# A hybrid decoder block on one core: the last expert chunk written out behind the loop, with the final norm beside it

## The chip, the cores and the metric

The kernel runs on one core of a Trainium2 chip. A core has TensorE (PE, matrix products), VectorE (DVE), ScalarE (ACT), GpSimd (POOL, which also issues gathers and scatters by index) and SyncE (SP, which here only issues DMAs); 16 DMA engines move the data. The engines run side by side, each works its own queue in order, and they wait for each other on semaphores. The metric is the device time of one execution in microseconds, the median of several runs.

## The reference

One decoder layer over 2048 tokens of width 1024, then a final norm:

```python
h = rmsnorm(x, norm_mix_w)
proj = h @ w_in                      # split into the inputs of two mixers
mixed = concat(gla(...), ssd(...))   # gated linear attention, state space scan
x = x + mixed @ w_out
h2 = rmsnorm(x, norm_ffn_w)
# 32 experts, each token goes to its top 4:
#   y = (clip(up) + 1) * (min(gate) * sigmoid(1.702 * gate)) @ w_down + b_down
x = x + moe_ffn(h2, ...)             # sum over the token's experts, weighted
return rmsnorm(x, final_norm_w)      # x * rsqrt(mean(x*x) + 1e-6) * w
```

All inputs and the output are float32.

## The kernel before

A first phase (mixers and router, about a third of the time) leaves two arrays in device memory: `xacc_d`, the residual stream, and `h2_d`, its normed rows. For each expert it also leaves a table of token numbers and gate weights.

The second phase is a loop over chunks. A chunk is one expert with up to 320 of its tokens; the chunks are sorted by size, and there is one loop for each of eight sizes (320, 304, ..., 208 tokens), all of them made by `chunk_loops`. In this run there are 32 chunks, and the last is of the smallest size, 208. A chunk `i` has 12 units of work, `q` = 0 to 11: units 0 to 7 are the gate and up products (128x416 and 128x208 products on `xhl`), units 8 to 11 the down products (on `ahl`). Each unit uses a 1 MB piece of weights. The precision of float32 is kept by splitting each operand in a high and a low part, and this takes three engines for each piece:

- SP: `load(e, q)` brings the piece into `raw`, a ring of four slots, once DVE has freed the slot (`v_lo`).
- ACT: `hi(i, q)` writes the high part `whi` from `raw`; DVE: `lo(i, q)` writes the low part `wlo`. Both run four units ahead of PE.
- PE: `products`; then ACT and DVE (`evict`) add the bias and the two halves. After each odd unit below 8, DVE computes the activation (`activated`), ACT its high part (`act_hi`) and DVE its low part (`act_lo`, `ahl`). The last quarter of unit 8 on PE waits for the last of these (`v_al`).

Between the units lie the token rows. `x_rows` on PE turns the gathered tokens of the NEXT chunk (in unit 8, and behind it); `x_evict`, `x_hi`, `x_lo` split them. `y_rows` turns the results `yT` of the PREVIOUS chunk back (behind units 1 and 2, in PSUM tile `tpm`), ACT scales them by the gate weights into `ybuf`, and POOL adds them to `xacc_d` by an indirect DMA (`scatter`, an accumulating write). There are two row blocks (128 and 80 rows for the smallest size), and POOL waits for the first scatter before it issues the second.

Behind the loop stands the tail: the results of the last chunk are turned (PE), scaled (ACT), scattered (POOL, two scatters one behind the other), and then SP loads all of `xacc_d` in four pieces of 2 MB into `fin` (line 590). For each of 16 tiles of 128 rows ACT squares and sums (`squares`, line 1243), POOL makes the root for four tiles at a time (lines 821 and 823: an add and a power), DVE scales (line 1827) and SP stores (line 594). `fin` takes 64 KB of each partition, which is free only when the expert buffers are.

`own_wait` (line 628) is a tiny POOL instruction in front of which POOL's waits stand.

## Time and profile before

| | us |
|---|---|
| median of 3 runs (3551.17 to 3553.92) | 3552.98 |
| the profiled execution | 3550.52 |
| its span in the trace | 3548.9 |
| PE busy (share of the span) | 3408.6 (96%) |
| DVE busy | 2147.0 (60%) |
| ACT busy | 1660.9 (47%) |
| POOL busy | 614.0 (17%) |

All times of rows are in microseconds from the start of the span. The times of the runs contain a little more than the span: 1.6 us around it in the profiled execution. In a timeline row the first number is the start, the second the duration, and a bracket says how long the engine was idle ahead of it and what ended that. "PEclk" is the TensorE clock that was granted, 1.00 being 2.4 GHz and 0.50 being 1.2 GHz; "DMA share" is the busy share of the 16 DMA engines.

### The profile page before, as it was taken

Reading aid. Unit: us, or ns where it says so; the run is one execution under the profiler, and the core shown is the slowest. Engines: PE = TensorE matmul, PEld = TensorE weight load, DVE = VectorE, ACT = ScalarE, POOL = GpSimd, SP = SyncE. Lnnn points to the kernel's source line nnn. Section 1 sums busy time; section 2 is a strip of 40 time slices with the busy share of each in tenths; the row PEclk is TensorE's granted clock in tenths of the full one; section 3 lists DMA queues with packets and bytes.
Section 4 is the critical chain, followed back from the end, with each engine's and each line's share of the span. In section 5 each row is a group of like instructions: output and inputs, shape, how many; then the busy total and the mean of one; then the engine's idle time right before and its main releaser. Section 6 shows DMA issues by size and latency. Waiting matters only on the chain.

```text
span 3548.9 us, 58966 instructions
## 1 busy us (share of the span) xinstructions
PE 3408.6 (96%) x22297; PEld 3153.4 (89%) x22297; DVE 2147.0 (60%) x2762; ACT 1660.9 (47%) x2161; POOL 614.0 (17%) x834
## 2 busy tenths in 40 slices
PE   5999999999996999999999999999999999999993
PEld 5888888888886999999999999988888999999992
DVE  3565355445455555555666666667667777777774
ACT  3443333333233444444444445455555556566664
POOL 1011111111113111111111211222112112112121
PEclk8999999999997999999999999999999999999996
DMA  9888888887865555665566666676666767768776
GB/s 340 332 306 333 299 292 286 298 306 269 300 253 187 170 169 172 180 182 178 180 191 183 205 191 188 185 218 211 203 199 214 215 204 235 223 205 242 237 235 244
DMA packets 474717, 821.53 MB, mean 231 GB/s; under 512 B 19408, under 2 KB 420960, under 8 KB 458224
## 3 DMA queue, kind: packets, MB, share of 16 engines
q1 hardware_dynamic: 442720, 716.52, 59.1%
q0 software_dynamic: 24400, 76.27, 9.3%
q10 hardware_dynamic: 7488, 27.27, 2.1%
q8 instruction: 70, 1.15, 0.1%
q14 instruction: 39, 0.32, 0.0%
HBM read 720.85 MB, written 99.16 MB: 231 GB/s over the span
## 4 chain that ended last, share of the span: by engine, by line
PE 94%; DMA 2%; DVE 2%; ACT 1%; issue 1%; POOL 0%; SPq 0%; DVEq 0%; ACTq 0%; POOLq 0%
PE acc L2272 22%; PE pp L1868 14%; PE acc L2274 11%; PE acc L2268 10%; PE acc L2270 10%; PE acc L2269 10%; PE pp L1858 5%; PE tpm L2250 2%; PE tpm L2244 2%; PE tp L1837 2%; DMA uraw<-in_w_in 1%; PE pm L1897 1%; PE seg L1913 1%; PE seg L1969 1%; PE pm L1988 1%
## 5 line engine op out<-in xcount | busy, mean ns | idle before, releaser
L1740 DVE TENSOR_TENSOR wlo<-raw,whi 128x2048 fp32r<-128x2048 f32 x388 | 887.8, 2289 | 302.6 <-ACT whi L1179 302.6
L2272 PE MATMUL acc<-xhl,whi 128*128 128x512 f32 (+3 forms) x2304 | 768.0, 386 | 2.3 <-ACT ybuf L1194 2.3
L1179 ACT ACTIVATE whi<-raw 128x2048 fp32r<-128x2048 f32 x388 | 741.5, 1911 | 22.9 <-DMA raw<-in_moe_w_gate 18.1
L628 POOL TENSOR_TENSOR gate_op<-gate_op 1x1 f32<-1x1 f32 x346 | 161.8, 468 | 2788.0 <-ACT ybuf L1194 869.2
L2274 PE MATMUL acc<-xhl,wlo 128*128 128x256 f32 (+3 forms) x2304 | 624.4, 271 | 0.0
L2268 PE MATMUL acc<-xhl,whi 128*128 128x272 f32 (+3 forms) x1792 | 534.7, 298 | 4.1 <-DVE xhl L1752 4.1
L2269 PE MATMUL acc<-xhl,whi 128*128 128x272 f32 (+3 forms) x1792 | 531.2, 296 | 0.0
L2270 PE MATMUL acc<-xhl,wlo 128*128 128x272 f32 (+3 forms) x1792 | 531.2, 296 | 0.0
L2272 PEld LDWEIGHTS acc<-xhl,whi 128*128 128x128 f32 x2304 | 432.0, 188 | 69.1 <-issue 2.5
L2274 PEld LDWEIGHTS acc<-xhl,wlo 128*128 128x128 f32 x2304 | 437.4, 190 | 0.0
L2272 PE MATMUL acc<-ahl,whi 128*128 128x512 f32 (+3 forms) x1152 | 387.6, 388 | 0.0
L2268 PEld LDWEIGHTS acc<-xhl,whi 128*128 128x128 f32 x1792 | 337.3, 188 | 4.3 <-issue 4.3
L1868 PE MATMUL pp<-u,hhi 128*128 128x512 f32 x1024 | 327.4, 401 | 10.3 <-DVE zb L1272 10.3
L2269 PEld LDWEIGHTS acc<-xhl,whi 128*128 128x128 f32 x1792 | 337.2, 188 | 0.0
L2270 PEld LDWEIGHTS acc<-xhl,wlo 128*128 128x128 f32 x1792 | 337.1, 188 | 0.0
L2274 PE MATMUL acc<-ahl,wlo 128*128 128x256 f32 (+3 forms) x1152 | 312.3, 271 | 0.0
L2268 PE MATMUL acc<-ahl,whi 128*128 128x272 f32 (+3 forms) x896 | 269.2, 300 | 0.0
L2269 PE MATMUL acc<-ahl,whi 128*128 128x272 f32 (+3 forms) x896 | 265.2, 296 | 0.0
L2270 PE MATMUL acc<-ahl,wlo 128*128 128x272 f32 (+3 forms) x896 | 265.1, 296 | 0.0
L1211 ACT ACTIVATE ubuf<-acc,bgu 128x256 f32<-128x256 f32 (+7 forms) x200 | 86.6, 470 | 349.2 <-PE acc L2270 195.4
L2272 PEld LDWEIGHTS acc<-ahl,whi 128*128 128x128 f32 x1152 | 216.0, 188 | 35.3 <-DVE ahl L1781 1.3
L1868 PEld LDWEIGHTS pp<-u,hhi 128*128 128x128 f32 x1024 | 191.7, 190 | 51.6 <-DVE zb L1272 10.4
(298 smaller groups left out, 5767.8 us busy)
## 6 DMA issues: line engine op xcount, KB each, us to landing
u<-split_d SPq DMA_DIRECT2D x112, 2048.0 KB, 8.8
raw<-in_moe_w_gate SPq DMA_DIRECT2D x130, 1024.0 KB
raw<-in_moe_w_up SPq DMA_DIRECT2D x130, 1024.0 KB
raw<-in_moe_w_down SPq DMA_DIRECT2D x128, 1024.0 KB
split_d<-u SPq DMA_DIRECT2D x16, 2048.0 KB, 10.7
uraw<-in_w_in SPq DMA_DIRECT2D x12, 1024.0 KB, 14.0
fin<-xacc_d SPq DMA_DIRECT2D x4, 2048.0 KB, 15.2
out<-fin SPq DMA_DIRECT2D x16, 512.0 KB, 8.3
```

Source lines behind the costliest of these rows:

```text
L628: pool.tensor_tensor(gate_op[0:1, 0:1], gate_op[0:1, 1:2], gate_op[0:1, 1:2], ALU.add).then_inc(gate_ran, 1)
L1179: act.activation(whi[:, q % RING, :, :], raw[:, q % RING, :, :], ACT.Copy).then_inc(a_hi, 1)
L1211: c = act.activation(into[:, b, 0:n], acc[:, q % 3, b, 0:n], ACT.Identity, bias=bias[:, b:b + 1])
L1740: dve.tensor_tensor(wlo[:, q % RING, :, :], raw[:, q % RING, :, :], whi[:, q % RING, :, :].bitcast(F32), ALU.subtract).then_inc(v_lo, 1)
L1837: i = pe.transpose(tp[:, b * P:(b + 1) * P], src(b), ident[:, :])
L1858: m = pe.matmul(pp[n % 2][:, c * PW:(c + 1) * PW], w_[:, k, c * P:(c + 1) * P], h_[:, k, :], start=(k == 0 and w_ is wh and h_ is hhi), st ...
L1868: m = pe.matmul(pp[t][:, :], h_[:, 4 * q + k, :], w_[:, k, :], start=(q == 0 and k == 0 and h_ is th and w_ is wh), stop=(q == 1 and k == ...
L2268: pe.matmul(into[:, 0:n], hi_, of[:, k, 0, 0:n], start=(k == 0), stop=False)
L2269: pe.matmul(into[:, 0:n], hi_, of[:, k, 1, 0:n], start=False, stop=False)
L2270: m = pe.matmul(into[:, 0:n], lo_, of[:, k, 0, 0:n], start=False, stop=(k == KD - 1))
L2272: pe.matmul(into[:, 0:2 * n].rearrange("p (c n) -> p c n", c=2), hi_, of[:, k, :, 0:n], start=(k == 0), stop=False)
L2274: m = pe.matmul(into[:, n:2 * n], lo_, of[:, k, 0, 0:n], start=False, stop=(k == KD - 1))
```

## The change

The last chunk leaves the loop: one is taken from the last loop's end, and the chunk is written out behind it as `chunk(i, SIZES[-1], True)`. In this copy:

- There is no next chunk, so its loads, high and low parts, gathers and turned tokens are gone.
- The results of the previous chunk are turned behind units 0 and 1 instead of 1 and 2.
- When those are scattered, SP starts to load `xacc_d` in pairs of tiles (`rows_in(p)`, two DMAs of 512 KB), into five pairs of buffers: `xg2` with `xraw1`, and the four slots of `raw` as they come free. ACT squares pair 0 in unit 6, pair 1 in unit 7, and so on to pair 5 in unit 11 (`norm_rows`), POOL makes the roots (`roots`), DVE scales pair 0 in unit 7 to pair 4 in unit 11 (`scaled_rows`), and SP stores them (`rows_done`). Pairs 5, 6 and 7 are loaded when the buffers of pairs 0, 1 and 2 have been stored.
- These rows lack the last chunk's contribution. Its own tokens are gathered apart from `xacc_d` (into `xg0`, `xg1`) after the scatters. When the last products are done, DVE adds the scaled result to them, ACT squares, POOL makes roots, DVE scales, and after all plain stores have landed POOL writes these rows to `out` with two indirect DMAs by the table.
- `fnw` (the weights of the norm) and `squares` get room of their own, and `fnw` is loaded at the start of the last chunk. In the first phase one small DVE step is added (the loop's end less one), and one small memset.

The core of the diff, SyncE first:

```diff
+            sp.dma_start(fnw[:, :], final_norm_w.partition_broadcast(P)).then_inc(d_fw, 16)
+            e = expert_of(sp, i)
...
+            def rows_in(p):
+                if p >= BUFS:
+                    sp.wait_ge(d_out[p - BUFS], 32)
+                for t in (2 * p, 2 * p + 1):
+                    sp.dma_start(rows_of_tile(t), xacc_d[t * P:(t + 1) * P, :]).then_inc(d_fin[p % BUFS], 16)
+
+            def rows_done(p):
+                sp.wait_ge(f_dve, 2 * p + (2 if p < 5 else 4 if p == 5 else 6))
+                for t in (2 * p, 2 * p + 1):
+                    sp.dma_start(out[0, t * P:(t + 1) * P, :], rows_of_tile(t)).then_inc(d_out[p % BUFS], 16)
+
+            sp.wait_ge(v_xl[1], i + 1)
             for r in range(2):
-                sp.wait_ge(v_xl[r], n_all + 1)
-            sp.wait_ge(v_lo, n_all * UNITS + RING)
...
+                sp.wait_ge(d_sc[r], i * 16 + 32)
             sp.wait_ge(d_sc[2], n_wide * 16 + 32)
-            for c in range(4):
-                sp.dma_start(fin[:, 4 * c:4 * c + 4, :],
-                             xacc_d[4 * c * P:4 * (c + 1) * P, :].rearrange("(t p) d -> p t d", p=P)).then_inc(d_fin[c], 16)
-            for t in range(TILES):
-                sp.wait_ge(f_dve, t + 1)
-                sp.dma_start(out[0, t * P:(t + 1) * P, :], fin[:, t, :]).then_inc(d_out, 16)
-            sp.wait_ge(d_out, 16 * TILES)
+            rows_in(0)
+            for q in range(RING):
+                sp.wait_ge(tiles_known, 1)
+                sp.wait_ge(v_lo, i * UNITS + (2 * RING + q + 1))
+                rows_in(q + 1)
+            rows_done(0)
+            for p in range(BUFS, PAIRS):
+                rows_done(p - BUFS + 1)
+                rows_in(p)
+            for p in range(PAIRS - BUFS + 1, PAIRS):
+                rows_done(p)
```

GpSimd:

```diff
+            for r in range(2):
+                pool.wait_ge(a_y[r], i + 1)
+                if r:
+                    pool.wait_ge(d_sc[0], i * 16 + 32)
+                next_own()
+                scatter(tabb, r, P)
+            pool.wait_ge(d_sc[1], i * 16 + 32)
...
+            for r, _, w in rows_of(n):
+                pool.indirect_dma_start(
+                    out=xg[r][0:w, :], out_offset=None, in_=xacc_d,
+                    in_offset=bass.IndirectOffsetOnAxis(ap=tabm[0:w, r, 0:1].bitcast(U32), axis=0)).then_inc(d_g[r], 16)
+
...
+            for p in range(6):
+                roots(2 * p, 2, 2 * p + 2, 2 * p + 1)
+            roots(TILES, 2, 14, 13)
+            roots(12, 4, 18, 15)
+            for b in range(BUFS):
+                pool.wait_ge(d_out[b], 64 if b < PAIRS - BUFS else 32)
+            pool.wait_ge(f_dve, 16)
+            next_own()
+            for r, _, w in rows_of(n):
+                pool.indirect_dma_start(
+                    out=out[0], out_offset=bass.IndirectOffsetOnAxis(ap=tabm[0:w, r, 0:1].bitcast(U32), axis=0),
+                    in_=ybuf[0:w, r, :], in_offset=None, bounds_check=SEQ - 1, oob_is_err=False).then_inc(d_last, 16)
```

ScalarE:

```diff
+            def norm_rows(p, ran):
+                act.wait_ge(d_fin[p % BUFS], 32 * (p // BUFS + 1))
+                for t in (2 * p, 2 * p + 1):
+                    act.wait_ge(f_act, ran + t - 2 * p)
+                    act.activation(squares[:, :], rows_of_tile(t), ACT.Square, scale=1.0 / 32.0,
+                                   accum_out=fst[:, t:t + 1]).then_inc(f_act, 1)
...
-                    hi(i, q + RING)
+                    if not final or q + RING < UNITS:
+                        hi(i, q + RING)
                     j = q // 2
+                    if final and q >= 6:
+                        norm_rows(q - 6, 2 * (q - 6))
...
                     if q < 8 and q % 2 == 1:
                         act_hi(i, n, j)
-                    if q == 1:
+                    row = q - (0 if final else 1)
+                    if row == 0:
...
+            _, i = chunk_loops(act, last, chunk, after_wide)
+            chunk(i, SIZES[-1], True)
+            for r, _, w in rows_of(SIZES[-1]):
+                act.wait_ge(f_dve, 11 + r)
+                act.wait_ge(f_act, 12 + r)
+                act.activation(squares[0:w, :], ybuf[0:w, r, :], ACT.Square, scale=1.0 / 32.0,
+                               accum_out=fst[0:w, TILES + r:TILES + r + 1]).then_inc(f_act, 1)
+            norm_rows(6, 14)
+            norm_rows(7, 16)
```

VectorE:

```diff
-                    lo(i, q + RING)
+                    if not final or q + RING < UNITS:
+                        lo(i, q + RING)
+                    if final and q >= 7:
+                        scaled_rows(q - 7, 2 * (q - 7) + 2)
...
+            chunk(i, n, True)
...
+            for r, _, w in rows_of(n):
...
+                dve.scalar_tensor_tensor(out=ybuf[0:w, r, :], in0=from_[0:w, :], scalar=tabm[0:w, r, 1:2].bitcast(F32),
+                                         in1=xg[r][0:w, :], op0=ALU.mult, op1=ALU.add).then_inc(f_dve, 1)
+            scaled_rows(5, 12)
+            dve.wait_ge(f_pool, 14)
...
+            for p in (6, 7):
+                scaled_rows(p, 16)
```

TensorE, the end:

```diff
+            chunk(i, SIZES[-1], True)
+            pe.wait_ge(a_y[1], i + 1)
+            y_whole(i + 1)
             y_rows(0)
-            pe.wait_ge(a_y[0], n_all + 1)
-            y_rows(1)
+            y_rows(1, acc[:, 0, :, :].rearrange("p b n -> p (b n)"))
```

How the rows of the queues move at three places. First ACT in units 6 and 7 of the last chunk (`gbuf` and `ubuf` are the results of the units, `whi` is `hi`, `sig` the sigmoid, `ahl` is `act_hi`). Before:

```order
L1211 ACTIVATE gbuf<-acc,bgu 128x208 [waits pe_u]
L1211 ACTIVATE gbuf<-acc,bgu 128x208
L1179 ACTIVATE whi<-raw 128x2048 [waits pe_u,d_raw2]
L1220 REGISTER_ALU
L1222 ACTIVATE sig<-gbuf 128x2x208 [waits a_e,v_e]
L1207 REGISTER_ALU
L1211 ACTIVATE ubuf<-acc,bgu 128x208 [waits pe_u]
L1211 ACTIVATE ubuf<-acc,bgu 128x208
L1179 ACTIVATE whi<-raw 128x2048 [waits pe_u,d_raw3]
L1187 REGISTER_ALU
L1188 ACTIVATE ahl<-act_v 128x2x208 [waits v_a]
```

The same stretch of ACT now:

```order
L1277 ACTIVATE squares,fst<-xg 128x1024 [waits f_act,d_fin0]
L1277 ACTIVATE squares,fst<-xraw 128x1024 [waits f_act]
L1289 REGISTER_ALU
L1291 ACTIVATE sig<-gbuf 128x2x208 [waits a_e,v_e]
L1266 REGISTER_ALU
L1270 ACTIVATE ubuf<-acc,bgu 128x208 [waits pe_u]
L1270 ACTIVATE ubuf<-acc,bgu 128x208
L1238 ACTIVATE whi<-raw 128x2048 [waits pe_u,d_raw3]
L1277 ACTIVATE squares,fst<-raw 128x1024 [waits f_act,d_fin1]
L1277 ACTIVATE squares,fst<-raw 128x1024 [waits f_act]
L1246 REGISTER_ALU
L1247 ACTIVATE ahl<-act_v 128x2x208 [waits v_a]
```

Two squares stand in front of the sigmoid, and two more in front of `act_hi`; each pair waits for a load.

Second, PE in unit 8 of the last chunk (the rows between two parts of the down products). Before:

```order
L2274 MATMUL acc<-ahl,wlo 128x208
L2313 ISA
L2244 MATMUL tpm<-ident,xg 128x128 [waits a_y1,d_g0]
L2244 MATMUL tpm<-ident,xg 128x128 x7
L2316 REGISTER_ALU
L2272 MATMUL acc<-ahl,whi 128x416 [waits v_al]
L2274 MATMUL acc<-ahl,wlo 128x208
```

And now:

```order
L2371 MATMUL acc<-ahl,wlo 128x208
L2369 MATMUL acc<-ahl,whi 128x416
L2371 MATMUL acc<-ahl,wlo 128x208
L2415 REGISTER_ALU
L2369 MATMUL acc<-ahl,whi 128x416 [waits v_al]
L2371 MATMUL acc<-ahl,wlo 128x208
```

The turned tokens that stood in front of the wait for `v_al` are gone; the wait has stayed.

Third, SP where the stores begin. Now:

```order
L594 DMA raw<-xacc_d 128x1024 [waits v_lo]
L594 DMA raw<-xacc_d 128x1024
L599 DMA out<-xg 128x1024 [waits f_dve]
L599 DMA out<-xraw 128x1024
L599 DMA out<-raw 128x1024 [waits f_dve]
L599 DMA out<-raw 128x1024
L594 DMA xg<-xacc_d 128x1024 [waits d_out0]
L594 DMA xraw<-xacc_d 128x1024
L599 DMA out<-raw 128x1024 [waits f_dve]
L599 DMA out<-raw 128x1024
L594 DMA raw<-xacc_d 128x1024 [waits d_out1]
L594 DMA raw<-xacc_d 128x1024
```

The load of pair 5 (the second `xg<-xacc_d`) stands behind the stores of pairs 0 and 1 and waits for the first of them to land; the load of pair 6 stands behind it. Before, four loads without a wait between them were followed by sixteen stores:

```order
L587 ISA
L588 ISA [waits d_sc1,d_sc0]
L590 DMA fin<-xacc_d 128x4x1024 [waits d_sc2]
L590 DMA fin<-xacc_d 128x4x1024 x3
L594 DMA out<-fin 128x1024 [waits f_dve] x16
L142 UNCONDITIONAL_BRANCH [waits d_out]
```
## Rows read from the trace of the kernel before

**Rows 1.** The chain that ended last, in order of time, tail.

```profile
3485.84 0.60 DVE yT L1763
...
3488.94 1.11 PE tpm L2250 x8
...
3492.05 6.21 DMA xacc_d<-ybuf,tabm
...
3499.06 5.93 DMA xacc_d<-ybuf,tabm
...
3506.12 17.47 DMA fin<-xacc_d
```

**Rows 2.** Timeline of PE: its last product.

```profile
3484.75 0.26 PE L2274 MATMUL acc<-ahl,wlo 128*128 128x208 f32 x1
```

**Rows 3.** Stretches: busy PE, PEld, DVE, ACT, POOL; PEclk; DMA share; GB/s.

```profile
3434.00:3439.00 5.00, 5.00 (x37) 4.97 (x36) 4.57 (x6) 3.66 (x4) 0.49 (x1) 1.00 0.00 0
...
3449.00:3454.00 5.00, 5.00 (x36) 4.97 (x35) 3.92 (x4) 3.00 (x4) 2.92 (x3) 1.00 1.09 355
...
3459.00:3464.00 5.00, 5.00 (x35) 4.97 (x34) 3.85 (x4) 3.00 (x4) 0.00 (x0) 1.00 0.98 317
...
3512.00:3518.00 6.00, 0.00 (x0) 0.00 (x0) 0.00 (x0) 4.26 (x8) 0.46 (x2) 0.50 1.00 401
```

**Rows 4.** Timeline of DVE, first phase: a step on one column.

```profile
1094.84 0.16 DVE L1720 TENSOR_TENSOR cv<-cv 128x1 f32<-128x1 f32 x1
```

**Rows 5.** Timeline of SP in the last chunk: the four down loads.

```profile
3438.95 11.63 SPq L502 DMA_DIRECT2D raw<-in_moe_w_down  x4
```

**Rows 6.** Timeline of POOL: scatters, and powers of the tail.

```profile
3449.10 1.11 POOL L628 TENSOR_TENSOR gate_op<-gate_op 1x1 f32<-1x1 f32 x1 [8.33 <-DMA xacc_d<-ybuf,tabb]
...
3499.06 1.56 POOL L760 DMA_INDIRECT xacc_d<-ybuf,tabm  x1 [0.46 <-issue]
...
3517.74 1.05 POOL L823 TENSOR_TENSOR fst<-fst,mhalf 128x4 f32<-128x4 f32 x1
...
3528.77 1.93 POOL L823 TENSOR_TENSOR fst<-fst,mhalf 128x4 f32<-128x4 f32 x1
```

**Rows 7.** Timeline of ACT in units 6 and 7 of the last chunk.

```profile
3459.26 0.76 ACT L1211 ACTIVATE gbuf<-acc,bgu 128x208 f32<-128x208 f32 x2 [1.17 <-PE acc L2274]
3459.90 1.92 ACT L1179 ACTIVATE whi<-raw 128x2048 fp32r<-128x2048 f32 x1
3461.71 0.55 ACT L1222 ACTIVATE sig<-gbuf 128x416 f32<-128x416 f32 x1
3464.05 0.76 ACT L1211 ACTIVATE ubuf<-acc,bgu 128x208 f32<-128x208 f32 x2 [1.80 <-PE acc L2274]
...
3467.13 0.55 ACT L1188 ACTIVATE ahl<-act_v 128x416 fp32r<-128x416 f32 x1 [0.52 <-DVE act_v L1776]
```

**Rows 8.** The tile `fin`: its instructions (min/median/max ns) and landings (us).

```profile
L1243 ACT ACTIVATE squares<-fin x16: 1039/1041/1057, 3513.1 to 3531.8; 128x1024 bf16<-128x1024 f32 x16
...
L1827 DVE SCALAR_TENSOR_TENSOR fin<-fin,fst,fnw x16: 1280/1280/1287, 3518.9 to 3539.1; 128x1024 f32<-128x1024 f32 x16
...
DMA to landing us min/median/max: 7.8/8.6/22.0
```

**Rows 9.** Groups by line from 3464 on: the tokens turned in unit 8.

```profile
L2244 PE MATMUL tpm<-ident,xg 128*128 128x128 f32 (+1 forms) x16 | 1.8, 256 | 0.0
```

**Rows 10.** Timeline of DVE in unit 10 of the last chunk: a low part.

```profile
3482.84 2.29 DVE L1740 TENSOR_TENSOR wlo<-raw,whi 128x2048 fp32r<-128x2048 f32 x1 [1.22 <-ACT whi L1179]
```

**Rows 11.** DMA issues by line: KB each, median us from issue to landing.

```profile
fin<-xacc_d SPq DMA_DIRECT2D x4, 2048.0 KB, 15.2
out<-fin SPq DMA_DIRECT2D x16, 512.0 KB, 8.3
...
fnw<-in_final_norm_w SPq DMA_DIRECT2D x1, 512.0 KB, 3.7
```

**Rows 12.** Stretches where the granted clock rises or falls, columns as above.

```profile
1120.00:1122.00 2.00, 2.00 (x12) 2.00 (x12) 2.00 (x2) 1.26 (x1) 1.84 (x2) 0.74 1.05 358
...
3493.00:3494.00 1.00, 0.00 (x0) 0.00 (x0) 0.00 (x0) 0.00 (x0) 0.61 (x1) 0.65 0.02 8
```

More of the change, by code:

```diff
@@ new lines, in roots @@
+            def roots(first, count, squares_done, n_):
+                a, b, c = (fst[:, k + first:k + first + count] for k in (0, TILES + 2, 2 * TILES + 4))
+                pool.wait_ge(f_act, squares_done)
+                next_own()
+                pool.tensor_tensor(b, a, epsx[:, 0:1].to_broadcast([P, count]), ALU.add).then_inc(f_pool, 1)
+                pool.wait_ge(f_pool, n_)
+                pool.tensor_tensor(c, b, mhalf[:, 0:count], ALU.pow).then_inc(f_pool, 1)
+            for p in range(6):
+                roots(2 * p, 2, 2 * p + 2, 2 * p + 1)
@@ L1224, in chunk @@
                         act_hi(i, n, j)
-                    if q == 1:
+                    row = q - (0 if final else 1)
+                    if row == 0:
                         act.wait_ge(p_tabb, i + 1)
-                    if q in (1, 2) or q == 3 and wide(n):
-                        y_rows(i, q - 1, tabb)
-                    if q in (7, 8) or q == 9 and wide(n):
+                    if row in (0, 1) or row == 2 and wide(n):
+                        y_rows(i, row, tabb)
+                    if not final and (q in (7, 8) or q == 9 and wide(n)):
                         x_hi(i + 1, q - 7, n)
@@ L1234, in after_wide @@
                 y_rows(i, 2, tabm)
-            _, n_all = chunk_loops(act, last, chunk, after_wide)
-            act.wait_ge(p_tabm, n_all)
-            for r in range(2):
-                y_rows(n_all, r, tabm)
-            for t in range(TILES):
-                if t % 4 == 0:
-                    act.wait_ge(d_fin[t // 4], 16)
-                act.activation(squares[:, t, :], fin[:, t, :], ACT.Square, scale=1.0 / 32.0,
-                               accum_out=fst[:, t:t + 1]).then_inc(f_act, 1)
+            _, i = chunk_loops(act, last, chunk, after_wide)
[7 more added lines that the diff above has]
+            norm_rows(7, 16)
         @block.vector
@@ L1720, in _ @@
             dve.tensor_tensor(sout[:, 1:2], sout[:, 1:2], bflat[:, 0:1], ALU.add).then_inc(sched_cols, 1)
+            step(dve.tensor_scalar(ends[:, SEGS - 1:], ends[:, SEGS - 1:], -1.0, None, ALU.add))
             step(dve.tensor_tensor_scan(last_of[:, :], ones[:, 0:KINDS], ends[:, E:SEGS:E + 1], 0.0, ALU.add, ALU.max))
@@ L1797, in _, with scaled_rows, chunk @@
             dve.wait_ge(v_one, 1)
-            def chunk(i, n):
+            def scaled_rows(p, roots_done):
+                if p == 0:
+                    dve.wait_ge(d_fw, 16)
+                dve.wait_ge(f_pool, roots_done)
+                for t in (2 * p, 2 * p + 1):
+                    k = 2 * TILES + 4 + t
+                    dve.scalar_tensor_tensor(out=rows_of_tile(t), in0=rows_of_tile(t), scalar=fst[:, k:k + 1],
+                                             in1=fnw[:, :], op0=ALU.mult, op1=ALU.mult).then_inc(f_dve, 1)
+            def chunk(i, n, final=False):
                 e = expert_of(dve, i)
@@ L2285, in y_whole, with chunk @@
                 pe.wait_ge(a_e, i * UNITS + PRIMED)
-            def chunk(i, n):
+            def chunk(i, n, final=False):
                 rows = rows_of(n)
@@ L2312, in chunk @@
                             products(q, n, b, range(6), ahl)
-                        pe.wait_ge(d_g[0], i * 16 + 32)
-                        pe.wait_ge(a_y[tail], i + 1)
-                        x_rows(0, n)
+                        if not final:
+                            pe.wait_ge(d_g[0], i * 16 + 32)
+                            pe.wait_ge(a_y[tail], i + 1)
+                            x_rows(0, n)
                         pe.wait_ge(v_al, i * 4 + 4)
@@ L2322, in chunk @@
                     m.then_inc(pe_u, 1)
-                    if q == 8 or q == 9 and wide(n):
+                    if not final and (q == 8 or q == 9 and wide(n)):
                         pe.wait_ge(tiles_known, 1)
```

106 lines of the change are left out of this document (60 added, 46 removed).

## Prediction

> **What bounds the kernel now.** I read the page's busy shares first (PE 96%), then the chain that ended last, in order of time, and there its end. Up to its last product PE is the chain almost without a gap; that product ends at 3485.0 [rows 2]. The span ends at 3548.9, so 63.9 us have no matrix work in them. The reader sees them as links of a chain in [rows 1]: the last add into yT and two sets of turned rows, a scatter of 6.2 us, a second of 5.9 us behind it, then the load of xacc_d, on which ACT waits 17.5 us for its third piece, then squares, roots, scales and stores. From 3512 on the DMA engines run at 401 GB/s with a share of 1.00 [rows 3]: 8.4 MB in and 8.4 MB out cannot go faster there. So there are two costs in the tail, the two scatters in series and 16.8 MB of traffic. Next I looked for room beside the last chunk. In the stretches of [rows 3] the DMA share is 0.00 at 3434 to 3439, but 1.09 and 0.98 at 3449 to 3454 and 3459 to 3464, since the four down pieces are issued together until 3450.6 [rows 5] and two scatters run there too. So the row traffic joins a queue that is full until about 3455, and has room behind it.
>
> **The change, part by part.** All times are on the axis of the profiled execution.
>
> *First phase.* One DVE step more on one column costs 0.16 us [rows 4], with its wait 0.2, on the way to the first chunk. The memset lies beside the first gathers. The loop's bodies are unchanged. Sum +0.2.
>
> *When the rows can start.* They need the previous chunk's scatters. The first now goes 4.8 us (one unit) earlier, into the stretch without DMA, and should take what the lone one took, 6.2 us [rows 1]. Before, it was issued at 3439.1, just behind the first down piece, and released POOL only at 3449.10 [rows 6], 10 us later. The second scatter now stands where that one stood: issued about 3441, landed 3451. SP is then free as well (3450.6), so pair 0 is issued at about 3451.3, the others when their ring slots are free: 3454.6, 3459.6, 3464.2, and pair 4 after the last low part, about 3473.
>
> *ACT and PE in units 6 to 8.* A pair of squares costs 2 x 1.04 [rows 8] plus a wait on the one before, 2.3 us. In unit 6 they stand ahead of the sigmoid, which starts at 3464.1 instead of 3461.7; eviction 7 then starts at 3464.65 instead of 3464.05 [rows 7]. In unit 7 they stand ahead of the high part of the activation: it ends at 3470.1 instead of 3467.7. Behind it wait DVE's low part (0.6 us, 3470.7) and, on PE, the last quarter of unit 8. PE gets there at 3467.6, since the 1.8 us of turned tokens [rows 9] that covered this wait are gone, and stalls 3.2 us. That quarter takes 1.2 us and ends at 3472.0; before, unit 9 began at 3470.6. So the last chunk becomes 1.4 us longer, not shorter: the removed 1.8 us are outweighed by a stall. The last product ends at 3486.4. This holds if pair 0 has landed by 3461.8 and pair 1 by 3467.2. Work queued ahead of pair 0 at 3451.3: about 4 us; then 2.6 us for each MB at 401 GB/s, with the two gathers between: pair 0 by 3460, pair 1 by 3464. No wait there.
>
> *Units 8 to 11.* ACT has 0.8 + 2.3 of 4.8 us to do, DVE 0.6 + 2 x 1.28 [rows 8]; the high and low parts that went (1.9 us in [rows 7], 2.3 us in [rows 10]) make room. Pairs 0 to 4 are scaled at about 3475.4, 3478.4, 3481.4, 3485.6 and 3490.3 and stored then.
>
> *The three late pairs.* Each waits for a store to land. A lone 512 KB load lands in 3.7 us [rows 11]; a pair adds 1.3 us, so 5.0 alone; beside other traffic I take 5 to 8.3 us, the upper end being the store of [rows 11]. With 5.5: pair 5 issued 3480.9, landed 3486 (needed 3487.5), pair 6 landed 3491 (needed 3494), pair 7 landed 3495 (needed 3496.3). Each is just in time. With 8.3 for each, pair 7 lands at 3498, 1.7 us late.
>
> *The tail.* The last add is done 1.4 us after the last product, as before (3486.4 against 3485.0 in [rows 1, 2]): 3487.8. Both sets of turned rows, now without ACT between them, take 2.2: 3490.1. DVE scales pair 4 until 3490.3 and adds both own blocks at 1.28: 3492.8. ACT squares the second own block until 3494.0 and pairs 6 and 7 until 3498.6. POOL's add and power take 1.05 us for the power alone and 1.93 beside a busy DVE [rows 6]; with the add and its gate I take 2.8: 3501.4. DVE scales four tiles in 4.9: 3506.3. The last pair's store, with nothing ahead, lands in 5.5: 3511.8 (bounds 5.0 and 8.3). POOL's gate 0.7: 3512.5; the first indirect write takes 1.56 and 0.3 to the next [rows 6], and the second lands 5.9 us after its issue at 3514.4 [rows 1]: 3520.3. Plain writes instead of accumulating ones could save up to 2 us, and rows dropped by the bound as well; I take none of it. End +0.4 and the first phase +0.2: the span is 3520.9 against 3548.9, that is -28.0 us.
>
> The Trainium skill ("DMA: Bandwidth & Descriptors", Anatomy of one DMA) fits a GpSimd DMA as 2.0 us plus bytes over 436 GB/s. The row of the accumulating scatter, 5.9 us for half a MB, is 2.7 us above the 3.2 us of that fit. By the page the last write would land 2.7 us sooner (3518.2, an estimate), by the row at 3520.9; the row is used.
>
> **The sum.** The profiled execution took 3550.5 with 1.6 around its span; the median lies 2.5 above it. 3552.98 - 28.0 = 3525.0.
>
> **The rivals.**
>
> *A convoy of loads.* Loads beside stores and weights land as the 2 MB pieces did, 15.2 us after issue [rows 11], not 5. Pair 0 then lands at 3466.5, 4.7 us after ACT asks, and PE loses that; the late pairs are issued after their stores (8.3 us) and land 15.2 us on: pair 7 at about 3509 instead of 3495, less 1.3 of slack, so +13, or +16 with part of the first delay. Time: 3541. For it: at 3449 to 3464 the engines are full [rows 3]. Against it: 15.2 is the median of pieces that queued behind each other, 8 MB at once.
>
> *The clock.* PE's stall of 3.2 us in unit 8 lets the granted clock fall to 0.50, and units 9 to 11 run on half clock for a while. In the trace the clock fell in 3493 to 3494 (mean 0.65) [rows 12], while PE's last work ended at 3490.1 [rows 1], so 3 us without work were followed by a fall. In the first chunk it came back at 1120 to 1122 (mean 0.74). Price: half of 2 to 4 us in the chain, +2; if it stays low for all three units (14.4 us of work), +14. Time: 3527 to 3539. The Trainium skill ("TensorE: Matmul & The Clock Gate", HAM oscillation) says that matmul runs cut by waits for DMA go cold each time; the trace shows a fall only behind the last product, so it neither bears that out nor excludes it. By that rule, applied once, the sum would be 3527.
>
> *ACT's queue stops the products (ends slower).* The place is the wait for pair 0 in unit 6, ahead of the sigmoid. If a load takes the longest landing in the trace, 22.0 us [rows 8], pair 0 lands at 3473.3: PE loses 11.5 us, and its clock falls (+2). The late pairs then cost 17 more than forecast, less 1.8 of slack: +15. Together +29: 3554, no gain left. It decides from a landing of about 21 us on; beyond 25 us the kernel is slower by over 7 us. Against it: 22.0 is the last of four pieces of 2 MB each.
>
> *The rows aren't really beside the chunk.* SP's queue is in order: if the scatters' semaphores come after 3465, the first five pairs start only with the last units, and one more round of 5 pairs (12 us of traffic) moves behind the chunk: 3537. For it speaks only the late release in [rows 6]; it would have to be 14 us later.
>
> **How the numbers follow.** Forecast 0.76 (own range 3517 to 3533). Convoy 0.12, clock 0.06, rows late 0.02, ACT's queue 0.04. The bounds of the forecast: last store +2.8, late pairs +1.7, squares that wait on each other +2, half a clock dip +1, against final writes -2.7 and roots at the short power -1.7. The range that leaves out 2 in 10, or a little less, is 3516 to 3539. A measurement of this kernel tells a difference above about 0.2%, 7 us, from none. Faster by over that is everything but ACT's queue: 0.95; within it 0.02; slower 0.03 (landings beyond 25 us, or a price in the unchanged loops that I don't see).
>
> **What would show it.** In the changed profile: the first row load of SP at 3451 (after 3458: the scatter step is wrong); no long wait of ACT's squares for a DMA in units 6 to 10 (over 2 us: the convoy); a PE wait of about 3 us on the low part of the activation in unit 8, and the last product at 3486; the granted clock at 1.00 in the stretches of units 9 to 11; ACT's waits for pairs 5, 6, 7 each below 2 us; the last plain store issued near 3507, landed near 3512, the two indirect writes behind it, and 34 to 35 us from the last product to the end. The prediction is wrong if that last stretch is above 45 us, or if the last product comes after 3492.

## The result, and the profile after

The changed kernel takes 3521.5 us (median of 4 runs, 3521.12 to 3522.08) against 3553.1 for the kernel before (4 runs, 3551.17 to 3553.92): ratio 0.9912, 95% interval 0.9899 to 0.9924, or 31.6 us less. The forecast was 3525.0, range 3516 to 3539. The two profiled executions differ by 28.4 us in their spans (3548.9 and 3520.5); the profiled one of before lay 2.5 us below its median, as the prediction noted, and that one of after 0.6 above, which is why the medians differ by more (31.6).

**How the traces are compared.** The first 3420 us, where nothing was changed but one small step and one small memset, end some us earlier or later from run to run: over all profiles of this study the first DVE copy of the last chunk (`bgu<-mcols`) starts between 3421.5 and 3433 us. So each stretch is counted from that copy, which is the mark below: from the mark to DVE's last add into yT (the chunk), and from there to the end of the span (the tail). Each count is read from one profiled execution. The changed kernel was profiled twice, and its two counts differ by 1.2 us in the chunk, 2.0 in the tail and 0.8 from the mark to the end (E8), so smaller differences between two kernels are not told from chance by these counts alone. In the changed kernel these are the two ends (min/median/max ns, first and last start in us):

```profile
L1882 DVE COPY bgu<-mcols x1: 168/168/168, 3429.9 to 3429.9; 128x16 f32 x1
...
L1835 DVE TENSOR_TENSOR yT<-yT,acc x4: 580/586/588, 3476.2 to 3491.3; 128x416 f32<-128x416 f32 x4
```

Before, the mark stands at 3428.7 and the last add at 3485.84 [rows 1]. The chunk took 57.1 us before and takes 61.4 after; the tail took 63.1 and takes 29.2. The change moved 33.9 us out of the tail, and gave 4.3 back in the chunk, where the forecast had 1.4.

**The tail.** The chain that ended last, in order of time (start, us):

```profile
3494.24 1.28 DVE ybuf L1916
...
3501.63 1.06 ACT squares L1277
3503.35 1.02 POOL fst L869
...
3509.67 4.27 DMA out<-raw
...
3515.04 1.07 POOL out L880
```

The two scatters and the load of [rows 1] are gone from it. What is left is what the prediction listed: own rows, squares, power, scales, the last plain store, the indirect writes.

**The start of the rows.** Timelines of POOL and of SP:

```profile
3442.24 0.18 POOL L651 TENSOR_TENSOR gate_op<-gate_op 1x1 f32<-1x1 f32 x1 [4.69 <-DMA xacc_d<-ybuf,tabb]
...
3452.44 0.18 POOL L651 TENSOR_TENSOR gate_op<-gate_op 1x1 f32<-1x1 f32 x1 [7.99 <-DMA xacc_d<-ybuf,tabb]
```

```profile
3452.44 0.35 SPq L594 DMA_DIRECT2D xg<-xacc_d  x1
...
3481.06 0.34 SPq L594 DMA_DIRECT2D xg<-xacc_d  x1
```

The first scatter, issued at 3435.97, released POOL 6.3 us later; the second, issued at 3442.89, took 9.5. The first row load starts in the very moment in which the second is done, at 22.5 us from the mark (forecast 22.6), and the load of pair 5 at 3481.06 (forecast 3480.9, read on an axis 1.2 us earlier).

**The chunk.** Timelines of ACT and of PE, then stretches (busy PE, PEld, DVE, ACT, POOL; granted clock; DMA share; GB/s):

```profile
3463.20 1.06 ACT L1277 ACTIVATE squares<-xg 128x1024 bf16<-128x1024 f32 x1 [0.19 <-DMA xraw<-xacc_d]
...
3470.55 0.53 ACT L1247 ACTIVATE ahl<-act_v 128x416 fp32r<-128x416 f32 x1
```

```profile
3471.76 0.71 PE L2369 MATMUL acc<-ahl,whi 128*128 128x416 f32 x1 [2.95 <-DVE ahl L1853]
```

```profile
3467.00:3469.00 2.00, 1.81 (x13) 1.55 (x11) 1.81 (x4) 2.00 (x2) 0.00 (x0) 1.00 1.03 406
3469.00:3471.00 2.00, 0.00 (x0) 0.00 (x0) 0.00 (x0) 1.97 (x5) 0.20 (x2) 1.00 0.26 104
3471.00:3473.00 2.00, 1.24 (x4) 1.21 (x5) 1.89 (x2) 0.08 (x1) 1.19 (x2) 0.55 0.00 0
3473.00:3475.00 2.00, 2.00 (x9) 1.95 (x8) 2.00 (x2) 0.56 (x2) 0.00 (x0) 0.50 0.09 18
3475.00:3477.00 2.00, 2.00 (x9) 1.93 (x9) 2.00 (x4) 1.97 (x4) 0.00 (x0) 0.50 0.95 358
3477.00:3479.00 2.00, 2.00 (x12) 1.96 (x12) 2.00 (x2) 0.42 (x2) 1.43 (x2) 0.74 1.03 408
3479.00:3481.00 2.00, 2.00 (x16) 1.99 (x15) 0.19 (x1) 0.05 (x1) 0.93 (x2) 1.00 1.03 422
```

The squares of pair 0 wait 0.2 us for their rows, not more; the second half of them landed 10.3 us after its issue. PE waits 2.95 us for the low part of the activation (forecast 3.2). Then comes what the forecast had not: the matmul behind the wait takes 0.71 us, where the same one takes 0.46 in E1 at full clock, the granted clock stands at half (1.2 GHz instead of 2.4) until about 3478, and PE gets through 9 matmuls in 2 us where it gets through 16 at full clock.

### The profile page after: what moved, and what is told of

It is laid out like the page before. It is cut to its first block, busy times and chain, and to the rows that moved or that the text cites. A ratio compares the mean times of both kernels' runs of the same rounds, so it can differ in the third digit from the quotient of the medians.

```text
span 3520.5 us, 58928 instructions
## 1 busy us (share of the span) xinstructions
PE 3413.2 (97%) x22281; PEld 3156.1 (90%) x22281; DVE 2138.2 (61%) x2760; ACT 1652.7 (47%) x2157; POOL 609.1 (17%) x845
## 4 chain that ended last, share of the span: by engine, by line
PE 94%; DMA 2%; DVE 2%; ACT 1%; issue 1%; POOL 0%; SPq 0%; POOLq 0%; DVEq 0%; ACTq 0%
PE acc L2369 22%; PE pp L1965 14%; PE acc L2371 11%; PE acc L2365 10%; PE acc L2366 10%; PE acc L2367 10%; PE pp L1955 5%; PE tpm L2347 2%; PE tpm L2341 2%; PE tp L1934 2%; DMA uraw<-in_w_in 1%; PE pm L1994 1%; PE seg L2010 1%; PE pm L2085 1%; PE seg L2066 1%
## 5 line engine op out<-in xcount | busy, mean ns | idle before, releaser
L1812 DVE TENSOR_TENSOR wlo<-raw,whi 128x2048 fp32r<-128x2048 f32 x384 | 878.5, 2288 | 300.9 <-ACT whi L1238 300.9
L1238 ACT ACTIVATE whi<-raw 128x2048 fp32r<-128x2048 f32 x384 | 733.6, 1911 | 23.8 <-DMA raw<-in_moe_w_gate 17.6
## 6 DMA issues: line engine op xcount, KB each, us to landing
xres<-in_x ACTq DMA_DIRECT2D x14, 512.0 KB, 10.2
```

The costliest lines, as they stand in the source:

```text
L1238: act.activation(whi[:, q % RING, :, :], raw[:, q % RING, :, :], ACT.Copy).then_inc(a_hi, 1)
L1812: dve.tensor_tensor(wlo[:, q % RING, :, :], raw[:, q % RING, :, :], whi[:, q % RING, :, :].bitcast(F32), ALU.subtract).then_inc(v_lo, 1)
```

## The experiments

All times below are medians; "from the mark" is read from the one profiled execution of each kernel. The ratios are to the kernel before as it was run beside each group: 3554.1 us for E1 to E4, 3555.0 for E5 to E8, 3554.6 for E9 and E10.

| kernel | time, ratio to before (95%) | chunk | tail | mark to end |
|---|---|---|---|---|
| before | 3553.1 | 57.1 | 63.1 | 120.2 |
| changed | 3521.5, 0.9912 (0.9899 to 0.9924) | 61.4 | 29.2 | 90.6 |
| E1 squares behind | 3519.2, 0.9897 (0.9882 to 0.9913) | 56.6 | 33.6 | 90.2 |
| E2 filler on PE | 3520.7, 0.9906 (0.9891 to 0.9922) | 58.2 | 30.9 | 89.1 |
| E3 peel alone | 3552.3, 0.9994 (0.9984 to 1.0003) | 56.3 | 63.4 | 119.7 |
| E4 no table write | 3515.9, 0.9894 (0.9879 to 0.9909) | 60.1 | 25.8 | 86.0 |
| E5 rows behind | 3539.9, 0.9960 (0.9946 to 0.9973) | 56.3 | 53.7 | 110.0 |
| E6 own buffers | 3512.6, 0.9885 (0.9870 to 0.9901) | 56.7 | 29.0 | 85.7 |
| E7 new order | 3512.8, 0.9880 (0.9865 to 0.9895) | 57.1 | 26.2 | 83.3 |
| E8 changed again | 3521.9, 0.9902 (0.9887 to 0.9917) | 60.3 | 31.1 | 91.4 |
| E9 all early | 3507.7, 0.9871 (0.9855 to 0.9888) | 57.1 | 24.0 | 81.1 |
| E10 old order | 3511.5, 0.9878 (0.9861 to 0.9894) | 56.6 | 29.2 | 85.8 |

**E1, squares behind the sigmoid and the high part.** PE's wait comes from ACT's squares that stand ahead of the activation. Here they stand behind it.

```
-                    if final and q >= 6:
-                        norm_rows(q - 6, 2 * (q - 6))
                     if q < 8 and q % 2 == 0:
...
                         act_hi(i, n, j)
+                    if final and q >= 6:
+                        norm_rows(q - 6, 2 * (q - 6))
```

> The changed kernel with one edit: in units 6 and 7 of the last chunk ACT's squares stand behind the sigmoid and behind the high part of the activation, not ahead of them. My theory: the stall of PE in unit 8 (2.9 us in the changed kernel's trace) falls to about 1.5, the granted clock stays at 1.00 behind it, which gives another 2.9 us back, and the last product and with it the end come 4 us sooner: 3517.5 us. The rival (the late pairs of rows and the DMA queue set the end, not the last product): PE ends 4 us sooner too, but the end moves by less than 1 us, 3521.

Timeline of PE, timeline of ACT, and the chain that ended last:

```profile
3467.65 0.46 PE L2369 MATMUL acc<-ahl,whi 128*128 128x416 f32 x1 [1.05 <-DVE ahl L1853]
```

```profile
3497.86 1.06 ACT L1277 ACTIVATE squares<-raw 128x1024 bf16<-128x1024 f32 x1 [4.51 <-DMA raw<-xacc_d]
```

```profile
3478.97 9.48 DMA out<-raw
...
3488.85 8.98 DMA raw<-xacc_d
```

The wait is down to 1.05 us, the clock stays at 1.00 in each stretch of 2 us from 3462 to 3484, and the chunk is 4.8 us shorter. But the end comes only 0.4 us sooner, which is not to be told from nothing, and so it is the rival's case: ACT now waits 4.5 us for the last pair of rows. Its load uses the buffer of pair 2 and starts when that store has landed, 9.5 us after its issue, and lands 9.0 us on. So the slower chunk of the changed kernel had hidden the chain of buffers; take the one away and the other sets the end. The profiles between the two fit this: ACT waits for pair 7 not at all with the chunk of 61.4 us, 1.1 to 2.0 us with those of 60.3 (E8), 60.1 (E4) and 58.2 (E2), and 4.5 here with 56.6.

**E2, something for PE to do in the gap.** 24 transposes of the identity, whose result nobody reads, ahead of the wait.

```
+                        if final:
+                            pe.wait_ge(a_y[1], i + 1)
+                            for k in range(24):
+                                pe.transpose(tpm[:, k % KD * P:k % KD * P + P], ident[:, :], ident[:, :])
                         pe.wait_ge(v_al, i * 4 + 4)
```

> The changed kernel with 24 turned copies of the unit matrix put on PE ahead of its wait in unit 8 (about 2.6 us of work that nobody reads, into a tile that is free). It leaves ACT's order and so the moment at which PE may go on as they are, and fills the wait. My theory: the wait as such costs 2.9 us and the clock that fell behind it another 2.9, so here the clock stays at 1.00 and the last product comes 2.9 us sooner: 3518.7 us. The rival (the slower products behind the wait have another cause, or the fall of the clock does not depend on this gap): the units behind it stay slow, 3521.5 us.

Timeline of PE, and two stretches:

```profile
3464.07 2.78 PE L2418 MATMUL tpm<-ident 128*128 128x128 f32 x24
3466.88 0.46 PE L2369 MATMUL acc<-ahl,whi 128*128 128x416 f32 x1
```

```profile
3466.00:3468.00 2.00, 1.98 (x15) 1.74 (x14) 1.77 (x2) 0.20 (x1) 1.31 (x3) 1.00 0.01 2
3468.00:3470.00 2.00, 2.00 (x16) 1.99 (x15) 2.00 (x2) 1.55 (x3) 0.00 (x0) 1.00 0.00 0
```

The last quarter of unit 8 starts at 41.5 us from the mark, as in the changed kernel (41.8): the wait is still there, PE only isn't idle in it. From that start to the last add it takes 16.7 us, as in E1 (16.7), against 19.6 in the changed kernel. So the fall of the clock cost 2.9 us in that profile, and the wait itself the other 1.6 to 1.9. This is the clean measurement of the clock, since no other instruction was moved; its size is not fixed, as two more profiles with the same wait show (1.6 us each, E4 and E8). The end came 1.4 us sooner, not 2.9; ACT waited 0.9 us for pair 5 and 1.9 for pair 7 here.

**E3, the peeled chunk alone.** The kernel before, with the last chunk written out without the next chunk's loads, splits and turned tokens, and with its old tail.

```
-            _, n_all = chunk_loops(pe, last, chunk, after_wide)
+            _, i = chunk_loops(pe, last, chunk, after_wide)
+            chunk(i, SIZES[-1], True)
+            n_all = i + 1
```

> The kernel before, with the last chunk written out behind the loop without its work for a next chunk (4 loads, high and low parts, gathers, turned tokens), and the old tail behind it. My theory: 1.8 us of turned tokens go, 0.7 us of wait on the activation's low part appears, the tail stays 64 us: 3552 us, 1 us below before. The rival (a good part of the gain is the dropped prefetch, whose 4 MB and ACT and DVE work slowed the end): 3545 us or less.

The chunk is 0.8 us shorter than before, with a PE wait of 0.8 us where the turned tokens stood; the time is not to be told from before (0.9984 to 1.0003). Dropping the work for a next chunk was worth next to nothing by itself: the rival (3545 or less) is out.

**E4, without the last indirect writes.** It leaves out the two writes by table, so that the 208 tokens of the last chunk keep the rows without that chunk's part.

```
-            for r, _, w in rows_of(n):
-                pool.indirect_dma_start(
-                    out=out[0], out_offset=bass.IndirectOffsetOnAxis(...), in_=ybuf[0:w, r, :], ...)
-            sp.wait_ge(d_last, 32)
```

> The changed kernel without the two indirect writes at its end: the last chunk's own tokens are computed but not stored, so their rows in the output stay without its contribution. My theory: the writes stand alone in series behind the last plain store (gate, two issues, landing), and the end comes 5.7 us sooner: 3515.8 us. The rival (the landing of the last stores and the end of the program cover part of it): 3519 us.

Timeline of PE, and the last plain store in the chain that ended last:

```profile
3463.40 0.46 PE L2364 MATMUL acc<-ahl,whi 128*128 128x416 f32 x1 [2.97 <-DVE ahl L1848]
```

```profile
3501.03 4.27 DMA out<-raw
```

From the landing of that store (3505.3) it takes 2.2 us to the end of the span (3507.5); in the changed kernel it takes 6.6 (3513.9 to 3520.5). So the writes cost 4.4 us, and not the 5.7 of the theory: as the rival had it, a part of the time behind the last store is there without them too. The median, 3515.9, falls on the theory's 3515.8 all the same, but the four runs lie between 3509 and 3519. From the mark the end comes 4.6 us sooner, 1.3 of it in the chunk: the wait of PE is the same (2.97), but from its end to the last add it takes 18.3 us instead of 19.6, the clock having fallen for a shorter time.

**E5, the rows behind the chunk.** The own rows stay apart; the loads of pairs 1 to 4 wait for the last product, and all squares and scales stand behind the chunk.

```
             rows_in(0)
+            sp.wait_ge(tiles_known, 1)
+            sp.wait_ge(pe_u, i * UNITS + UNITS)
```

> The changed kernel, but the norm of the rows stands behind the last chunk: the loads of pairs 1 to 4 wait for PE's last product (pair 0's load alone stays early), and all squares and scales stand behind the last unit on ACT and DVE. The own rows stay apart and are written by table. Theory (two separate gains): the chunk has no extra work, so its last add comes about 57 us after the start of the last chunk's first DVE copy, as before (57.1), and PE's wait on the low part of the activation is below 1 us with the clock at 1.00. The two scatters in series (12 us) are gone from the tail, but its 16.8 MB of traffic are back: with 10 row buffers and loads that wait for stores about 45 to 50 us from the last add to the end, against 63.1 before and 29.2 after. Time about 3539, half of the gain. Rival (the gain is the scatters alone, the rows are near free in the chunk's shadow or not): the tail stays at 29 to 35 us and the time is within 5 us of the changed kernel's 3521.5. Second rival (reusing few buffers makes a chain of load, squares, scale, store for each pair): the tail is 60 us or more and the time about that of before.

Two steps of the chain that ended last:

```profile
3501.66 8.97 DMA out<-raw
...
3511.03 7.07 DMA raw<-xacc_d
```

110.0 from the mark: 9.7 less than E3, which has the scatters in series, and 19.4 more than the changed kernel, which has the rows beside the chunk. So of the gain of the change over E3 (29.1 from the mark) one third came with the own rows kept apart and two thirds with the row work (loads, squares, scales, stores) put beside the products. This is a split of the steps and not a clean price of each cost: the two scatters took 13 us in [rows 1], but E5 pays for them with reused buffers, which E3 does not have (ACT waits 8.05 us for pair 5), and with the writes by table. The time, 3539.9, was forecast at 3539; the tail of 53.7 is 4 to 9 longer than forecast, as each reused buffer costs a store and a load of 7 to 9 us. That the time fits although the tail does not is chance: against the kernel before, the count from the mark gives 10.2 us and the medians give 15.1.

**E6, more row buffers.** E1, and seven pairs of buffers for eight pairs of rows.

```
+        rows_at += [xraw[0][:, :, :].rearrange("p k n -> p (k n)"), ybuf[:, 2, :]]
         rows_at += [raw[:, q, k:k + 4, :]... for q in range(RING) for k in (0, 4)]
+        rows_at += [units_[:, k * D:(k + 1) * D] for k in range(2)]
```

> The kernel with the squares behind the sigmoid and the high part of the activation, and seven row buffers for the eight pairs instead of five: pair 1 has a free block of the turned tokens and the third block of ybuf, pair 6 the unit buffers once the activation is done; only pair 7 reuses the buffer of pair 0. Theory (in the kernel with the squares behind, the end was set by pair 7, whose load waited for the store of pair 2): pair 7's load is issued at about 55 us after the start of the last chunk instead of 60.7, ACT waits under 1 us for it instead of 4.5, and the end comes 3 to 4.5 us sooner: 86 to 87 us from the start of the last chunk to the end instead of 90.2, time about 3515. Rival (the DMA engines are full, an earlier issue only moves the queue): ACT waits as long for pair 7, 89.5 to 90.5 from the start of the chunk to the end.

Timeline of ACT, pair 7:

```profile
3489.06 1.06 ACT L1277 ACTIVATE squares<-xg 128x1024 bf16<-128x1024 f32 x1
```

No wait is left before it, and the end comes 4.5 us sooner than in E1, at 85.7. Behind the last add ACT's only long idle time is 2.0 us for the own rows, and then six squares run without a gap: now they set the end.

**E7, another order of the row work.** E6 with the squares of pairs 0 to 7 in units 6, 7, 8, 8, 9, 10, 10, 11, the scales earlier as well, and the own rows behind them.

```
+                        for p in {6: (0,), 7: (1,), 8: (2, 3), 9: (4,), 10: (5, 6), 11: (7,)}.get(q, ()):
+                            norm_rows(p, 2 * p)
```

> The kernel with seven row buffers, and the work on the rows in an order that ends earlier: squares of pair 0 in unit 6, 1 in unit 7, 2 and 3 in unit 8, 4 in unit 9, 5 and 6 in unit 10, 7 in unit 11, roots by pairs, scales of 0 to 5 in units 7 to 11, and then the own rows, pairs 6 and 7, the own rows' scale. Theory (what is left behind the last add is a chain of ACT's squares, roots, scales and stores, and most of it can stand in the chunk): about 20 to 22 us from the last add to the end instead of 29 to 34; 79 to 82 us from the start of the last chunk to the end; time 3508 to 3511. Rival (the traffic sets the end: 16.8 MB of rows at 401 GB/s are 42 us, behind the last weights, so that nothing ends before about 75 us and the loads come too late for their squares): ACT and with it the evictions wait for rows in units 8 to 11, the last add comes 2 to 6 us later and the end at 84 to 90 us, 3513 to 3520.

Timeline of ACT, and the chain that ended last:

```profile
3488.02 1.06 ACT L1276 ACTIVATE squares<-xg 128x1024 bf16<-128x1024 f32 x1 [4.78 <-DMA xraw<-xacc_d]
```

```profile
3471.06 9.34 DMA out<-xraw
...
3480.80 7.19 DMA xraw<-xacc_d
```

Forecast 79 to 82, measured 83.3, and in time nothing against E6 (2.3 us less from the mark). The chunk did not get longer (57.1), so the rival's place was wrong, but its cause was half right: the one reused buffer is again on the path. The store of pair 0 lands 9.3 us after its issue although it was the first store, with 14 of the 16 row loads issued ahead of it; and while SP waits for it, the stores of pairs 2 to 5 stand behind that wait.

**E8, the changed kernel again.**

> The changed kernel once more, beside the others on one chip. It should stand at a ratio of 0.991 to the kernel before and at 90 to 91 us from the start of the last chunk to the end, with PE's wait of 2.9 us on the low part of the activation and the granted clock at about 0.5 for 6 to 8 us behind it. If the clock stays at 1.00 this time, the fall is not tied to that wait, and the last add comes about 3 us sooner.

```profile
3470.71 0.45 PE L2369 MATMUL acc<-ahl,whi 128*128 128x416 f32 x1 [3.11 <-DVE ahl L1853]
```

```profile
3471.00:3473.00 2.00, 2.00 (x11) 1.96 (x11) 2.00 (x2) 0.52 (x2) 0.22 (x1) 0.69 0.00 0
3473.00:3475.00 2.00, 2.00 (x9) 1.93 (x8) 2.00 (x2) 1.97 (x4) 0.00 (x0) 0.50 0.53 156
3475.00:3477.00 2.00, 2.00 (x14) 1.99 (x14) 2.00 (x4) 0.46 (x2) 1.37 (x2) 0.95 1.02 395
```

The wait and the fall come again, but the fall is shorter than the 6 to 8 us expected: about 3.5 us at half clock, and 18.3 us from the end of the wait to the last add, so 1.6 lost instead of 2.9. All in all 91.4 from the mark, because the tail is 2.0 us longer; here ACT did wait for pair 7:

```profile
3499.96 1.06 ACT L1277 ACTIVATE squares<-raw 128x1024 bf16<-128x1024 f32 x1 [1.98 <-DMA raw<-xacc_d]
```

**E9, all loads early.** E7 with eight pairs of buffers: no load waits for a store.

```
+            more = ma("more", [D])
+        rows_at += [more[:, :]]
+            rows_in(7)
-                if p == 1:
-                    sp.wait_ge(d_out[0], 32)
-                    rows_in(7)
```

> The kernel with the new order of the row work, and now eight pairs of row buffers of their own: no row load waits for a store. Theory (in the kernel before, ACT waited 4.8 us for pair 7, whose load stood behind the store of pair 0): pair 7's load is issued at about 47 us after the start of the last chunk instead of 54.6, ACT has no wait for a row load behind the last product, its last square ends at about 62 us after that start instead of 66.4, and the end comes 3.5 to 4.5 us sooner: about 79 us from the start of the last chunk instead of 83.3; time about 3508.5. Rival (the traffic sets the end by now): loads and stores fill the engines up to the last plain store anyway, with stretches at 250 to 310 GB/s in them, the last plain store lands less than 1.5 us sooner, and the end stays at 82 to 84 us.

The chain that ended last, and the stretch in front of its end:

```profile
3491.86 1.21 DVE more L1875
...
3493.46 6.94 DMA out<-more
```

```profile
3484.00:3494.00 10.00, 1.95 (x14) 1.55 (x12) 9.05 (x8) 3.39 (x6) 7.02 (x7) 0.55 1.02 419
```

81.1 from the mark, 2.2 less than E7: between theory (79) and rival (82 to 84). ACT waits for no row load. The last scale is done 67.3 us from the mark, DVE being busy in 9.05 of the last 10 us, and the last store then takes 6.9 instead of 4.3, since the engines still work off the stores before it at 419 GB/s. So the stores that queue up cost 2.6 us of the end here. What less arithmetic alone would bring was not run.

**E10, eight pairs of buffers, the old order.** E6 with the buffers of E9; the diff is that of E9.

> The same eight pairs of buffers, but squares, roots and scales in the order of the changed kernel (only behind the sigmoid and the high part of the activation). Theory (ACT's chain of squares behind the own rows sets the end here, not a buffer): ACT had no wait for pair 7 in the kernel with seven pairs of buffers, so nothing changes: 85 to 86.5 us from the start of the last chunk to the end, time about 3512.5. With the run beside it this separates order from buffers: the order alone is then worth 6 us once nothing waits. Rival (the buffers are what counts, the order is worth nothing): both of these kernels end within 1 us of each other, counted from the start of the last chunk.

85.8, as E6 (85.7): an eighth buffer is worth nothing where no wait points at it. Against E9 the order is worth 4.7 us from the mark once nothing waits, and 3.8 in the medians; 6 was forecast.

**The best version is E9:** 3507.7 us (3505.48 to 3513.59), ratio 0.9871 (0.9855 to 0.9888) to the kernel before, beside it on one chip. Its interval does not touch that of the changed kernel (0.9899 to 0.9924) and just meets that of E8 (0.9887 to 0.9917); those of E9 and E10 overlap, and only the counts from the mark tell the two apart.

## Why the prediction was right, and where it was not

*The bound.* Two costs in the tail, scatters in series and 16.8 MB of traffic. E5 shows that both steps gain, 9.7 us with the own rows apart and 19.4 with the row work beside the products; it does not price the scatters or the traffic by themselves.

*Start of the rows.* Scatter 6.3 us (forecast 6.2), first row load at 22.5 us from the mark (22.6). Right.

*PE's wait in unit 8.* 2.95 and 3.11 us for a forecast of 3.2, caused by the squares ahead of the activation: E1 moves them and the wait falls to 1.05. Right in mechanism and size.

*The clock.* This is the step that failed. The forecast let units 9 to 11 run at full clock and gave the rival "clock" 0.06, for the reason that the trace of before showed a fall only behind the last product. That was a misreading. The row of that fall spoke for the rival, 3 us without matmuls being followed by it [rows 12], and the same trace has others, among them one ahead of the first chunk, where PE had just waited 2.0 and 0.4 us, and one in the first phase without any wait of PE around it. Stretches of before:

```profile
554.00:556.00 2.00, 2.00 (x14) 2.00 (x14) 0.49 (x4) 0.38 (x1) 0.00 (x0) 0.60 0.99 420
```

```profile
1074.00:1076.00 2.00, 0.60 (x4) 0.52 (x4) 1.07 (x6) 0.94 (x1) 1.77 (x3) 1.00 0.21 86
1076.00:1078.00 2.00, 1.65 (x8) 1.30 (x8) 1.34 (x8) 0.48 (x3) 1.39 (x3) 0.66 0.49 195
```

The price, 2.9 us by E2 and 1.6 in the profiles of E4 and E8, lies at or below the lower end of the rival's bounds (2 to 14). The Trainium skill ("TensorE: Matmul & The Clock Gate", HAM oscillation) had the rule that matmul runs cut by waits for DMA go cold each time. Here the clock fell in all three profiles with the long wait in unit 8 (2.95, 2.97 and 3.11 us), which was one for ACT and DVE; behind another wait of 2.3 us it fell in seven of twelve profiles (last section). The chunk became 4.3 us longer instead of 1.4.

*The tail.* Forecast 33.7 from the start of the last add, measured 29.2. The path was the forecast's; four of its terms were too large or too small: POOL's add and power 1.6 instead of 2.8 (-1.2), the last store 4.7 from the end of DVE instead of 5.5 (-0.8), POOL's gate behind it +0.4, and the indirect writes 5.5 from the issue of the first to the end instead of 8.4 (-2.9). The last is the term that was mis-sized: the row of the accumulating scatter of 128 rows, 5.9 us [rows 1], was used for a plain write of 80. DMA issues of the changed kernel from 3400 on (median us to landing):

```profile
out<-raw SPq DMA_DIRECT2D x12, 512.0 KB, 4.4
...
xacc_d<-ybuf,tabb POOLq DMA_INDIRECT x2, 7.8
...
out<-ybuf,tabm POOLq DMA_INDIRECT x2, 3.4
```

The plain one lands in 3.4 us, the first of 128 rows as well as the second of 80, so it is the kind of write and not its size that counts here; the other kernels of the study that have it show 3.4 or 3.5. The prediction had named this as "up to 2 us" and taken none. The fit of the Trainium skill ("DMA: Bandwidth & Descriptors", Anatomy of one DMA), an estimate of 3.2 us for 128 rows, was the nearer one; it does not hold for the accumulating scatter (6.3 us, and 9.5 beside the weights).

*The late pairs.* No wait of ACT for pairs 5, 6 and 7 in the first profile, as forecast, but with less reason than it seemed: the clock's 2.9 us gave the loads time. In the second profile (E8) pair 7 came 2.0 us late, and in E1, with the shorter chunk, 4.5. The forecast's 5.5 us fits neither kind: in the first profile the stores that a load waits for landed in 4.3 to 4.7 us and the three late loads in 5.9, 7.2 and 8.4; in E1 a store took up to 9.5 and a load up to 10.3. So the rival "convoy" was in part true and covered up.

*The sum.* In spans -28.0 was forecast and -28.4 measured: +1.2 in front (the mark, chance from run to run), +4.3 in the chunk, -33.9 in the tail. The errors of +2.9 in the chunk and -4.5 in the tail stand against each other. The number is closer than its parts, and that is luck. In medians 31.6 us were gained against 28.0 forecast.

*The other rivals.* "ACT's queue stops the products" did not come: pair 0 was 0.2 us late (0.3 in E8), though with that the 1.8 us that the forecast had to spare were used up. "Rows not beside the chunk" did not either; E5 shows what it would have cost, 110.0 instead of 90.6 from the mark (the prediction had 12 us for it, where the whole shift costs 19.4).

## What to carry to other kernels

When work of a tail moves beside products, look first at what stands behind it in the queue of the engine that takes it: 2.3 us of squares ahead of one activation cost PE 1.9 us of waiting and 1.6 to 2.9 of half clock, and behind it next to nothing (chunk 56.6 against 56.3 in E3). The gaps of PE of about 3 us in this kernel were each followed by a stretch at 1.2 GHz, so such a gap is worth a price of its own in a forecast. Then take away waits one after the other and look at the mark-to-end time each time: here each fix (E1, E2) gave less than its own gain until the next constraint, reused buffers and then the order, was taken away too.

## What the runs showed of the hardware

- The clock's fall behind a gap is not the same each time: gaps of 2.95, 2.97 and 3.11 us (changed, E4, E8) led to about 6, 3.5 and 3.5 us at half clock, gaps of 1.04 to 1.06 (E1, E6, E7, E9, E10) and of 0.7 to 0.8 (E5, E3) to none. In the middle of the program, on code that no edit touched, PE waits 2.3 us for ACT in every profile. Behind that wait, or in it, the clock fell in seven of them (changed, E3, E4, E5, E6, E9, E10) and stayed in five (before, E1, E2, E7, E8); the kernel of the first and of E8 is the same. Timeline of PE and a stretch, changed kernel, then E8:

```profile
2274.08 0.76 PE L2369 MATMUL acc<-xhl,whi 128*128 128x512 f32 x1 [2.36 <-ACT ybuf L1253]
```

```profile
2275.00:2277.00 2.00, 2.00 (x8) 1.71 (x7) 0.00 (x0) 0.00 (x0) 1.28 (x1) 0.50 0.60 187
```

```profile
2275.38 0.47 PE L2369 MATMUL acc<-xhl,whi 128*128 128x512 f32 x1 [2.33 <-ACT ybuf L1253]
```

```profile
2277.00:2279.00 2.00, 2.00 (x14) 1.72 (x13) 0.00 (x0) 0.00 (x0) 0.61 (x1) 1.00 0.90 258
```

- This can be only one source of the differences in front of the mark: E4, with the fall, has the earliest mark (3421.5), and before, without it, one of 3428.7. The rest stays open.
- An indirect write of half a MB without accumulation landed in 3.4 us, one with it in 6.3 alone and 9.5 beside weight loads.
- Where row loads and stores mix, the DMA engines are sometimes full and move less. In E1, when the first stores met the late loads (the clock at 1.00, share and GB/s in the last two columns):

```profile
3476.00:3478.00 2.00, 2.00 (x16) 1.98 (x15) 2.00 (x2) 0.92 (x2) 0.93 (x2) 1.00 1.03 416
3478.00:3480.00 2.00, 2.00 (x16) 1.99 (x15) 0.81 (x2) 1.26 (x3) 1.09 (x2) 1.00 1.10 260
```

The cause of that dip was not looked into and stays open.
